# Mixture of experts on one core: tokens gathered without padding, and the order of the expert products

## The reference

```python
def hier_moe(h, rg_w, rg_b, re_w, re_b, w_gate, w_up, w_down):
    ...
    e_w = g_w * e_w / jnp.sum(e_w, axis=-1, keepdims=True)
    eid = g_idx * EXPERTS_PER_GROUP + e_idx
    comb = jnp.sum(jax.nn.one_hot(eid, N_EXPERTS, dtype=jnp.float32) * e_w[..., None], axis=1)
    y = jnp.zeros_like(h)
    for e in range(N_EXPERTS):
        he = jax.nn.silu(h @ w_gate[e]) * (h @ w_up[e])
        y = y + comb[:, e:e + 1] * (he @ w_down[e])
    return y
```

## Time and profile before

| what | value |
|---|---|
| median of 3 runs | 1428.33 us (1427.76 to 1431.74) |
| the profiled execution's own time | 1429.39 us |
| its span, first to last instruction | 1427.6 us |
| TensorE matmuls busy, whole span | 1322.8 us (93%), 9406 |
| VectorE, ScalarE, GpSimd busy | 886.2, 599.7, 38.2 us |
| expert pairs, first gate product to last down product | 1172.75 to 1412.03 us |
| TensorE busy from 1205 to 1380 us | 175.00 of 175 us |
| transfers of 1 MiB from 1176 us on | 82, for duos 7 to 47 |

### The profile page before, as it was taken

How to read it: one execution, slowest core, us unless ns; L and a number is a source line. 1 busy time by engine, 2 the same in 40 slices (tenths; PEclk the granted TensorE clock), 3 DMA queues, 4 the chain that set the end, 5 groups by cost and what they waited for, 6 DMA issues and landing times.

```text
span 1427.6 us, 22974 instructions
## 1 busy us (share of the span) xinstructions
PE 1322.8 (93%) x9406; PEld 1150.0 (81%) x9406; DVE 886.2 (62%) x1428; ACT 599.7 (42%) x957; POOL 38.2 (3%) x53
## 2 busy tenths in 40 slices
PE   7999999899999899998989999969899859999995
PEld 6999889798898899987979899868788746566563
DVE  3999867855555599986785555566964652222223
ACT  4346673444444334666344444434454322212211
POOL 1000000000000000000000000020240000000000
PEclk9999999999999999999999999989999979999998
DMA  9754434465555365443546555644546639999980
GB/s 294 250 180 140 143 95 156 136 234 190 176 181 200 118 207 165 149 141 91 176 133 229 177 189 193 196 136 148 151 137 229 222 121 391 417 416 412 420 356 32
DMA packets 172585, 290.00 MB, mean 203 GB/s; under 512 B 10324, under 2 KB 143076, under 8 KB 160204
## 3 DMA queue, kind: packets, MB, share of 16 engines
q1 hardware_dynamic: 169580, 281.55, 56.6%
q0 software_dynamic: 2752, 7.07, 1.7%
q10 hardware_dynamic: 160, 0.08, 0.0%
HBM read 287.61 MB, written 3.16 MB: 204 GB/s over the span
## 4 chain that ended last, share of the span: by engine, by line
PE 68%; DVE 23%; ACT 5%; issue 3%; DMA 1%; POOL 0%; DVEq 0%; SPq 0%; ACTq 0%; POOLq 0%
PE ps L1615 15%; PE ps L1616 15%; PE ps L1617 15%; PE ps L2051 8%; DVE w_lo L1047 7%; DVE cvh L1162 5%; PE ps L2073 4%; ACT w_hi L667 3%; PE ps L2035 2%; PE ps L2082 2%; DVE nm L1120 1%; DVE gT L1087 1%; DVE x_nat L1093 1%; PE ps L1630 1%; DVE ro L1154 1%
## 5 line engine op out<-in xcount | busy, mean ns | idle before, releaser
L1047 DVE TENSOR_TENSOR w_lo<-raw,w_hi 128x2048 fp32r<-128x2048 f32 (+2 forms) x166 | 372.3, 2243 | 170.0 <-ACT w_hi L667 169.9
L667 ACT ACTIVATE w_hi<-raw 128x2048 fp32r<-128x2048 f32 (+2 forms) x166 | 309.2, 1863 | 247.4 <-PE ps L1617 240.9
L1615 PE MATMUL ps<-xT_hi,w_lo 128*128 128x256 f32 (+1 forms) x1184 | 341.3, 288 | 1.5 <-DVE xT_lo L1299 1.5
L1616 PE MATMUL ps<-xT_lo,w_hi 128*128 128x256 f32 (+1 forms) x1184 | 335.1, 283 | 0.0
L1617 PE MATMUL ps<-xT_hi,w_hi 128*128 128x256 f32 (+1 forms) x1184 | 334.9, 283 | 0.0
L1615 PEld LDWEIGHTS ps<-xT_hi,w_lo 128*128 128x128 f32 (+1 forms) x1184 | 226.4, 191 | 10.2 <-issue 9.4
L1616 PEld LDWEIGHTS ps<-xT_lo,w_hi 128*128 128x128 f32 (+1 forms) x1184 | 226.6, 191 | 0.4
L1617 PEld LDWEIGHTS ps<-xT_hi,w_hi 128*128 128x128 f32 (+1 forms) x1184 | 226.4, 191 | 0.0
L1615 PE MATMUL ps<-w_hi,xT_lo 128*128 128x256 f32 (+2 forms) x544 | 165.0, 303 | 1.9 <-DVE w_lo L1047 1.6
L1616 PE MATMUL ps<-w_lo,xT_hi 128*128 128x256 f32 (+2 forms) x544 | 162.2, 298 | 0.0
L1617 PE MATMUL ps<-w_hi,xT_hi 128*128 128x256 f32 (+2 forms) x544 | 162.2, 298 | 0.0
(11 more groups left out here) (387 smaller groups left out, 2025.3 us busy)
## 6 DMA issues: line engine op xcount, KB each, us to landing
raw<-in_w_in SPq DMA_DIRECT2D x72, 1024.0 KB, 5.2
raw<-in_w_ff SPq DMA_DIRECT2D x64, 1024.0 KB, 5.2
raw<-in_w_gate SPq DMA_DIRECT2D x10, 1024.0 KB, 7.4
raw<-in_w_up SPq DMA_DIRECT2D x10, 1024.0 KB, 8.9
w_exp<-in_w_down SPq DMA_DIRECT2D x10, 1024.0 KB, 9.9
raw<-in_w_o SPq DMA_DIRECT2D x8, 1024.0 KB, 4.9
w_exp<-in_w_gate SPq DMA_DIRECT2D x8, 1024.0 KB, 9.0
raw<-in_w_down SPq DMA_DIRECT2D x8, 1024.0 KB, 10.7
```

The lines of the kernel that those rows point to most:

```text
L667: nc.scalar.activation(split_of(u)[0][:, 0:n], raw[:, u % RAW, 0:n], ACT.Copy).then_inc(hi_done, 1)
L1047: nc.vector.tensor_tensor(split_of(u)[1][:, 0:n], raw[:, u % RAW, 0:n], split_of(u)[0][:, 0:n].bitcast(F32), ALU.subtract).then_inc(split_ ...
L1615: nc.tensor.matmul(out_, left[1], right[0], start=start, stop=False)
L1616: nc.tensor.matmul(out_, left[0], right[1], start=False, stop=False)
```

## The change

1. **A first round of its own** (`r is None`); the further rounds keep the old scheme. The first quad (pairs 0 and 1) is gathered as before. All 512 assignments are also gathered once, expert after expert with no gaps. VectorE's `seat_tokens` forms each expert's start `off` by a scan over the counts, finds each token's two seats with `max`, and builds `one_hot` (256 x 512) by two compares and two fused compare-and-adds. TensorE's `pack(k)` (8 calls, 4 matmuls of 512 columns each) multiplies the tokens with it, and ScalarE's `pack_copy` stores to `packed`. The 28 woven gathers and their copies are gone.
2. **GpSimd** reads each expert's start into registers and copies 64 columns from there into the slots `xg_slots` (128 partitions x 8 x 64), two copies to a pair from pair 2 on. It waits until the up product of pair p-2 is done; the gate product of pair p waits for it (`slots_put`).
3. **Order on TensorE.** The gate product of pair p+1 now stands between the turn and the down product of pair p, into a second PSUM bank. `place_slots(p+1)` stands ahead of the up product of pair p. The duos are loaded in the new order of use (`FIRST`). Four packs and `place_slots(1)` stand ahead of the first up product, four packs behind it.
4. **Layout.** `lnb`, `E`, `pT` and `ro` become one tensor `wide`, so that `packed` fits over them; `place` has 3 buffers; one more small table is loaded by GpSimd's queue.

```diff
+FIRST = [(0, 0), (0, 1)] + [x for p in range(PAIRS - 1) for x in ((p + 1, 0), (p, 2), (p + 1, 1))] + [(PAIRS - 1, 2)]
+PLACES = 3
...
+            pool.dma_start(seats, t["c_slots"].partition_broadcast(P)).then_inc(slots_in, 16)
+
+            pool.wait_ge(pos_ready, BASE)
+            for p in range(2, PAIRS):
+                at = [pool.value_load(base_i[0:1, 2 * p + e:2 * p + e + 1], min_val=0, max_val=BANK - CAP) for e in range(2)]
+                if p == 2:
+                    pool.wait_ge(gath_c, 4 + KC)
+                pool.wait_ge(duo_used, duo_at(None, p - 2, 1) + 1)
+                for e in range(2):
+                    last = nc.gpsimd.tensor_copy(xg_slots(p, e), packed[:, :, bass.ds(at[e], CAP)])
+                last.then_inc(slots_put, 1)
...
+            nc.vector.memset(off[:, 0:1], 0.0)
...
+                def seat_tokens():
+
+                    then(nc.vector.tensor_tensor_scan(off[:, 1:N_EXPERTS], ones[:, 0:1].broadcast_to([P, N_EXPERTS - 1]), ps[:, ACC, 0:N_EXPERTS - 1], 0.0, ALU.mult, ALU.add))
+                    then(nc.vector.tensor_tensor(seat, pos, bc(off, 1, TT), ALU.add))
+                    for a in range(TT):
+                        last = nc.vector.max(two[:, a], seat[:, a])
+                    then(last)
+                    for a in range(TT):
+                        last = nc.vector.tensor_scalar(one_hot[:, a, :], seats, two[:, a, 0:1], None, ALU.is_equal)
+                    then(last)
+                    for a in range(TT):
+                        last = nc.vector.scalar_tensor_tensor(out=one_hot[:, a, :], in0=seats, scalar=two[:, a, 1:2], in1=one_hot[:, a, :].bitcast(F32), op0=ALU.is_equal, op1=ALU.add)
+                    last.then_inc(pos_ready, 1)
...
+                def pack(k):
+
+                    if k == 0:
+                        pe.wait_ge(pos_ready, HOT)
+                    if k >= 4:
+                        pe.wait_ge(gath_c, 4 + k - 3)
+                    for i, x in enumerate((h2_hi, h2_lo)):
+                        for a in range(TT):
+                            last = nc.tensor.matmul(ps[:, ACC + k % 4, :], x[:, a, k * P:(k + 1) * P], one_hot[:, a, :], start=i == 0 and a == 0, stop=i == 1 and a == TT - 1)
+                    last.then_inc(gathered, 1)
...
+                if r is None:
+                    for n in range(4):
+                        gather(n)
+                    place_slots(0)
+                    inner(0, 0)
+                    for k in range(4):
+                        pack(k)
+                    place_slots(1)
+                    inner(0, 1)
+                    for k in range(4, KC):
+                        pack(k)
+                    for p in range(PAIRS):
+                        if p >= 1:
+                            if p + 1 < PAIRS:
+                                place_slots(p + 1)
+                            inner(p, 1)
+                            scatter(p - 1)
+                        turn_he(p)
+                        if p + 1 < PAIRS:
+                            inner(p + 1, 0)
+                        outer(p)
```

More of the change, by code:

```diff
@@ L283, in build @@
         summed, shifted = sem("summed"), sem("shifted")
+        slots_put = sem("slots_put")
+        POS, HOT, BASE = 1, 2, 3
         dve_link2 = sem("dve_link2")
@@ L1545, in place_slots @@
                 def place_slots(p):
-                    q = p % 2
[L1548 to L1554, removed]
-                    nc.vector.tensor_scalar(slot_ids, slot_ids, float(CAP), None, ALU.add).then_inc(shifted, 1)
-                    dve.wait_ge(shifted, r + 1)
@@ L1558, in moe_round @@
[L1558 to L1572, removed]
+                    q = p % PLACES
@@ L1582, in moe_round @@
                         nc.vector.tensor_tensor(y_lo[h], ps[:, Y_BANKS[h], :], y_hi[h].bitcast(F32), ALU.subtract).then_inc(y_lod[h], 1)
+                if r is None:
+                    pick_tokens(0)
+                    dve.wait_ge(comb_ready, 2)
+                    weigh_picks(0)
+                    seat_tokens()
+                    place_slots(0)
+                    dve.wait_ge(more_ready, 1)
+                    rounds_left.append(dve.value_load(more[0:1, 0:1]))
+                    for p in range(PAIRS):
+                        if p + 1 < PAIRS:
+                            place_slots(p + 1)
+                        swish(p)
+                        if p % 2 == 0 and p + 2 < PAIRS:
+                            pick_tokens(p // 2 + 1)
+                            weigh_picks(p // 2 + 1)
+                        low_sums(p)
+                else:
+                    nc.vector.tensor_scalar(slot_ids, slot_ids, float(CAP), None, ALU.add).then_inc(shifted, 1)
+                    dve.wait_ge(shifted, r + 1)
+                    pick_tokens(0)
+                    weigh_picks(0)
+                    pick_tokens(1)
+                    for p in range(PAIRS):
+                        if p % 2 == 0 and 1 <= p // 2 < QUADS - 1:
+                            pick_tokens(p // 2 + 1)
+                        place_slots(p)
+                        if p % 2 == 1 and p < PAIRS - 1:
+                            weigh_picks(p // 2 + 1)
+                        swish(p)
+                        low_sums(p)
                 for h in range(2):
@@ L2014, in _ @@
             for a in range(TT):
-                last = nc.tensor.matmul(ps[:, 7, 64:96], ones[:], member[:, a, :], start=a == 0, stop=a == TT - 1)
+                last = nc.tensor.matmul(ps[:, ACC, 0:N_EXPERTS], ones[:], member[:, a, :], start=a == 0, stop=a == TT - 1)
             last.then_inc(rt_mm, 1)
@@ L2060, in place_slots, with turn_he @@
                     last.then_inc(place_T, 1)
+                def turn_he(p):
+                    pe.wait_ge(he_ready, plus(p + 1, PAIRS))
+                    for c in range(2):
+                        last = nc.tensor.transpose(gate_up(r, p)[:, c * P:(c + 1) * P], he[:, p % 2, c * P:(c + 1) * P], ident[:])
+                    last.then_inc(heT_done, 1)
                 def outer(p):
-                    d = 3 * p + 2
+                    d = duo_at(r, p, 2)
                     duo_arrived(pe, r, d)
@@ L2076, in scatter @@
                 def scatter(p):
+                    if r is None and p == 0:
+                        pe.wait_ge(gath_c, 4 + KC)
                     for h in range(2):
@@ L2081, in scatter @@
                             for k, y in enumerate((y_lo[h], y_hi[h])):
-                                last = nc.tensor.matmul(ps[:, ACC + 2 * a + h, :], place[p % 2][:, a, :], y, start=p == 0 and k == 0, stop=p == PAIRS - 1 and k == 1)
+                                last = nc.tensor.matmul(ps[:, ACC + 2 * a + h, :], place[p % PLACES][:, a, :], y, start=p == 0 and k == 0, stop=p == PAIRS - 1 and k == 1)
                             if p == PAIRS - 1 and a == 0:
@@ L2085, in scatter @@
                         last.then_inc(scattered[h], 1)
-                if r is not None:
-                    pe.wait_ge(summed, r + 1)
[L2089 to L2105, removed]
+                if r is None:
+                    for n in range(4):
+                        gather(n)
+                    place_slots(0)
+                    inner(0, 0)
+                    for k in range(4):
+                        pack(k)
+                    place_slots(1)
+                    inner(0, 1)
+                    for k in range(4, KC):
+                        pack(k)
+                    for p in range(PAIRS):
+                        if p >= 1:
+                            if p + 1 < PAIRS:
+                                place_slots(p + 1)
+                            inner(p, 1)
+                            scatter(p - 1)
+                        turn_he(p)
+                        if p + 1 < PAIRS:
+                            inner(p + 1, 0)
+                        outer(p)
+                else:
+                    pe.wait_ge(summed, r + 1)
+                    for n in range(4):
+                        gather(n)
+                    for p in range(PAIRS):
+                        inner(p, 0)
+                        place_slots(p)
+                        inner(p, 1)
+                        if p // 2 < QUADS - 1:
+                            gather(4 + 2 * p)
+                        if p >= 1:
+                            scatter(p - 1)
+                        turn_he(p)
+                        if p // 2 < QUADS - 1:
+                            gather(5 + 2 * p)
+                        outer(p)
                 scatter(PAIRS - 1)
```

113 lines of the change are left out of this document (79 added, 34 removed).

## The result

The changed kernel takes 1412.01 us (median of 4 runs, 1409.66 to 1416.89) against 1428.92 (4 runs, 1427.76 to 1431.74): a ratio of 0.9874, 95% interval 0.9854 to 0.9895. It is faster by about 18 us. Forecast were 1412.6 us and a range of 1407.5 to 1420.5. The profiled run has a span of 1407.8 us, 19.8 under the one of before. Where these 19.8 us come from is read piece by piece, since only one piece is the forecast one.

A forecast was written before the change was run, and what follows sets the result against it. Expert stage: TensorE and the DMA engines both full. TensorE runs 13.3 us a pair until transfers at 5.05 us a duo catch it; end 1396.3 instead of 1412.03, -15.7: span 1411.9, median 1412.6, range 1407.5 to 1420.5 us.

The forecast's parts named there:

- gate product of pair 0 done: Start of the expert stage: a memset (+0.1) and place 0 (+0.37) move its end from 1176.35 to 1176.8 us.
- a pair of TensorE: TensorE's place, up, scatter, turn, gate and down for one pair: 13.27 us, taken as 13.3, against 15.16 before.
- duo 47 complete: Last weight transfer: lands at 1391.3 us, 38 duos of 5.05 us after duo 9 at 1199.4.
- end if TensorE set it: Last down product without transfer limits: 1195.6 + 14 x 13.3 + 10.1 = 1391.9 us.
- a copy on GpSimd: GpSimd's copy into the slots: 1.33 us, bounds 0 to 2.83, costing nothing up to 7.8 us a copy.
- seats done on VectorE: `seat_tokens` keeps VectorE busy from 1167.76 to about 1172 us, free by nearly 5 us before the packs.
- 29.4 us of gathers: The 28 woven gathers on TensorE: 2.10 us a pair in 14 pairs, all of it on the path.
- The delay of duo 9: Weight transfers: packs delay the first slot releases, so duo 9 completes at 1199.4 against 1196.9, 2.5 us later.
- The pace of 5.05 us a duo: DMA engines' own pace for the weights: 38 duos in 191.8 us, 15.14 us a pair.
- rival A: TensorE sets the pace to the end, with duos at 4.9 us or less: -20.1, 1408.2 us; chance 0.14.
- rival C: GpSimd's copies hold VectorE's activation, 1.8 us of stall in each of 15 pairs: 1435.2 us; chance 0.09.
- The tail: What follows the last down product (last split, last scatter, norm, store): unchanged.

The follow-up runs named there:

- half the weights: Changed kernel loading only the first half of each matrix from duo 7 on; median 1405.5 us, stage 224.1 us.
- a ring of six: Changed kernel with a ring of 6 duos instead of 7; ratio 0.9922, stage 234.05 us.
- the old order: Changed kernel with the gather without padding kept, but products and duo loads in the order of the kernel before; stage 233.2 us, 4.0 longer.
- 64 memsets: Kernel before with 64 one-column memsets added on VectorE behind the picks; a pause of 2.25 us is there, one instruction later.
- the eightfold one: Changed kernel with each pair of GpSimd copies made 8 times over; stage 229.1 us, no change.

## Why the prediction was right, point by point

Times are us from the first gather, so that the start of the stage drops out; "forecast" counts from 1167.04.

| step | forecast | measured |
|---|---|---|
| gate product of pair 0 done | 9.8 | 9.5 |
| duo 8 asked for | 17.5 | 17.2 |
| duo 9 asked for, complete | 25.0, 32.4 | 25.0, 32.4 |
| a pair of TensorE | 13.27 | 13.26 |
| duo 47 complete | 224.3 | 223.9 |
| end of the stage | 229.3 | 229.2 |
| end if TensorE set it | 224.9 | 224.1 (half the weights) |
| a copy on GpSimd | 1.33 (0 to 2.83) | 0.62 |
| seats done on VectorE | 5.0 | 3.8 |
| behind the stage | unchanged | -2.4 |

*Gathers, packs, pair.* The pair came out as read from the earlier trace rows, the packs at 3.9 for four instead of 3.7. The activation is ready before the turn. That all 29.4 us of gathers lie on the path was read too high, 28.2 do; the forecast sum did not use the figure.

*The transfers.* The step that carries the forecast is that the queue, full at 417 GB/s, gives back part of the gain. Three runs bear it out: half the weights (-5.1), a ring of six (+4.9), the old order (+4.0 of 9.2). TensorE waits for weights in the last three pairs alone, as forecast. The delay of duo 9, the term that the sum uses, was right to 0.1 us as well. The pace of 5.05 us a duo was right as a sum: 38 duos from 1197.8 to 1389.3 are 5.04. Its reading was coarse. Duo by duo the landings come every 4.97 us in every trace with whole matrices, also in the one of before, and single pauses are strewn in: four behind duo 11 before, 3.4 us together, and in the changed kernel two, 1.3 us at duo 11 and 1.5 at duo 40. So rival A's argument, that 5.05 contains pauses, was right in kind, but the deeper queue hardly filled them, and its end at 224.9 was out of reach even without any: 229.2 - 2.8 = 226.4.

*GpSimd.* Costs nothing, as forecast; the copy is half as long as taken, and the row that spoke against rival C (L1376 beside L643) named what sets the activation apart.

*Missed.* The tail, 2.4 us, put down as unchanged. Without it the same stage would have given about 1414.4, also in range. That the median hit within 0.6 us is partly luck: the span was forecast as 1411.9 and came out at 1407.8, but it stands 0.7 under the median of the runs in one kernel and 4.2 in the other, and the two misses cancel.

## What to carry to other kernels

Where two resources are both full, read two numbers before shortening the one on the path: the other's pace, and how early its results lie ready; the gain is cut where the two meet, here after 15.8 of 20.9 us. When a ring is full and its engine idle, the time until the queue fills counts as much as the pace, and moving work between the first releases moved the gap here and hardly shortened it, until it was spread over four intervals. Put a helper engine's work beside operations that take an operand from PSUM, and compare stretches, not spans: the part of a few us in front and behind may belong to other things.

## What the runs showed of the hardware that was not expected

- **A deep queue slows the issuer.** With releases ahead of the transfers, the time to landing grew from 7.1 to 28.5 us. With ten transfers of 1 MiB issued and not landed, most issues took SyncE 2.13 us (one 5.3) instead of 0.33 to 0.43; a transfer takes 2.48. It cost nothing, as the DMA engines stayed full.
- **Pauses.** In otherwise even landings single gaps of 0.3 to 1.6 us appear, in one trace (64 memsets) of 2.1. One of them is worth as much as moving the packs. They are not strewn at random: the two traces of the changed kernel and the eightfold one have them at the same duos, 11 and 40, and in each of these six gaps one instruction fetch of 16 KB starts. But in the trace of the changed kernel nine more such fetches between 1200 and 1388 us bring no gap. What makes the gaps stays open; the fetches are a candidate.
- **A branch can cost 2.4 us** by where the code lies, and twelve unrelated instructions removed it.
